# Post-norm transformer step with routed experts: norm, modulation, logits and choice of experts done token tile by token tile

## The reference

```python
xs = layer_norm(ALPHA * xs + g1 * y, ln1_g[l], ln1_b[l])
f = moe_ffn(xs * (1.0 + sc2) + sh2, w_router[l], b_router[l], w_expert_gu[l],
            w_expert_down[l], w_shared_gu[l], w_shared_down[l])
xs = layer_norm(ALPHA * xs + g2 * f, ln2_g[l], ln2_b[l])
```

```python
scores = jax.nn.sigmoid((x @ w_router).astype(jnp.float32))
sel = scores + b_router.astype(jnp.float32)
grp_score = lax.top_k(sel.reshape(t, N_GROUPS, N_EXPERTS // N_GROUPS), 2)[0].sum(-1)
_, gidx = lax.top_k(grp_score, TOPK_GROUPS)
gmask = jax.nn.one_hot(gidx, N_GROUPS, dtype=jnp.float32).sum(1) > 0
emask = jnp.repeat(gmask, N_EXPERTS // N_GROUPS, axis=1)
_, eidx = lax.top_k(jnp.where(emask, sel, NEG_INF), TOP_K)
```

## Time and profile before

| what | value |
|---|---|
| median of 3 runs | 2039.12 us (2036.37 to 2043.51) |
| the profiled execution | 2030.75 us, its span 2029.0 us |
| PE busy | 1544.4 us, 76% |
| DVE busy | 562.2 us, 28% |
| ACT busy | 317.1 us, 16% |
| POOL busy | 195.8 us, 10% |
| mean DMA rate | 284 GB/s |
| mean granted clock | 0.858 |

### The profile page before, as it was taken

One profiled execution on the slowest core, in us unless ns is written; L12 is line 12 of the kernel. 1 busy time (PEld: TensorE's weight loads), 2 busy tenths in 40 slices (PEclk: granted clock), 3 DMA queues, 4 the chain that ended last, 5 costly groups with the idle time before them and its releaser, 6 DMA issues. The chain is left out here.

```text
span 2029.0 us, 20342 instructions
## 1 busy us (share of the span) xinstructions
PE 1544.4 (76%) x7609; PEld 791.7 (39%) x7609; DVE 562.2 (28%) x1126; ACT 317.1 (16%) x620; POOL 195.8 (10%) x196
## 2 busy tenths in 40 slices
PE   3797888795976878877338979987958768788663
PEld 1685563542322323322116856645423323233221
DVE  0534435621110111101615253355201111111116
ACT  0322450110000000000012234411100000010000
POOL 0000000141010110110000000002401101111000
PEclk7898799697987988989768987996979888899887
DMA  7534418179999999996475344182799999999964
GB/s 291 189 108 165 170 22 322 69 252 424 411 408 417 408 403 390 401 424 239 186 278 160 125 148 163 42 325 77 283 423 405 416 406 397 415 398 397 403 243 173
DMA packets 114674, 576.90 MB, mean 284 GB/s; under 512 B 41644, under 2 KB 44220, under 8 KB 73480
## 3 DMA queue, kind: packets, MB, share of 16 engines
q1 hardware_dynamic: 93992, 534.35, 66.3%
q0 software_dynamic: 20512, 41.09, 5.4%
q10 hardware_dynamic: 64, 0.07, 0.0%
HBM read 565.09 MB, written 40.39 MB: 298 GB/s over the span
## 5 line engine op out<-in xcount | busy, mean ns | idle before, releaser
L993 PE MATMUL bank<-ring,arena_a 128*32 128x512 f32 (+2 forms) x2432 | 518.3, 691 | 218.0 <-DMA ring<-in_w_expert_gu 213.8
L993 PEld LDWEIGHTS bank<-ring,arena_a 128*32 128x32 f32 (+2 forms) x2432 | 175.4, 145 | 528.1 <-issue 527.1
L1017 PE MATMUL bank<-arena_b,arena_a 128*32 128x512 f32 (+2 forms) x800 | 207.4, 601 | 12.6 <-DMA arena_b<-in_w_expert_down 11.5
L1497 DVE SCALAR_TENSOR_TENSOR arena_a<-arena_a,slot_w,bank 128x256 f32<-128x256 f32 x64 | 30.8, 480 | 658.1 <-ACT arena_a L1737 631.8
L1737 ACT ACTIVATE arena_a<-bank 128x256 f32<-128x256 f32 x64 | 24.7, 385 | 915.5 <-PE bank L993 896.7
L1793 POOL DMA_INDIRECT scratch_y<-arena_a,slot_idx x64 | 63.6, 994 | 917.1 <-DVE arena_a L1514 915.9
L778 PE MATMUL bank<-win_hi,xmT_hi 128*128 128x512 f32 (+1 forms) x288 | 110.8, 385 | 26.0 <-DVE arena_a L1141 23.4
L1017 PE MATMUL bank<-arena_a 128*32 128x512 f32 (+2 forms) x416 | 116.0, 595 | 0.0
L1513 DVE COPY arena_a<-bank 128x512 f32<-128x512 f32 x64 | 44.3, 692 | 249.0 <-PE bank L1017 249.0
L779 PE MATMUL bank<-win_hi,xmT_lo 128*128 128x512 f32 (+1 forms) x288 | 111.2, 386 | 0.0
L780 PE MATMUL bank<-w_lo,xmT_hi 128*128 128x512 f32 (+1 forms) x288 | 110.7, 384 | 0.0
(11 more groups left out here) (266 smaller groups left out, 1667.2 us busy)
## 6 DMA issues: line engine op xcount, KB each, us to landing
ring<-in_w_expert_gu SPq DMA_DIRECT2D x128, 2048.0 KB
arena_b<-in_w_expert_down SPq DMA_DIRECT2D x88, 1024.0 KB, 22.3
ring<-in_w_mod SPq DMA_DIRECT2D x24, 2048.0 KB
arena_a<-in_w_expert_down SPq DMA_DIRECT2D x40, 1024.0 KB
ring<-in_w_in SPq DMA_DIRECT2D x10, 2048.0 KB
ring<-in_w_out SPq DMA_DIRECT2D x4, 2048.0 KB
ring<-scratch_y SPq DMA_DIRECT2D x4, 2048.0 KB, 10.8
ring<-scratch_y SPq DMA_DIRECT2D x8, 1024.0 KB, 17.1
```

Of the source, the lines that this page charges most:

```text
L993: ins = pe.matmul(psum[b % 2][r:r + w, :], xT[:, k, r:r + w], ring_view(gu_slot(n))[:, k, :], start=(k == 0), stop=(k == KD - 1))
L1017: ins = pe.matmul(psum[5 + f][r:r + w, :], hT[b % 2][:, k, r:r + w], down[n % ND][:, k, CH * f:CH * f + CH], start=(k == 0), stop=(k == 1))
```

## The change

The work is reordered by tiles; what is computed stays the same.

- `norm` takes a third argument, `follow`, and calls it for tile t right behind that tile's `scale_shift`. In the first norm this is the modulation, in the last norm the residual. Each waits for ScalarE's normalisation of its tile. ScalarE's `norm` is not changed.
- TensorE multiplies the logits of tiles 0 and 1 together into one bank, then turns tile 2 and multiplies its logits into another. ScalarE copies tiles 0 and 1, does their sigmoid, copies tile 2, does its sigmoid.
- `choose(t)` does the whole choice of one tile; every operation works on that tile alone. The mask's semaphore counts three, and TensorE waits for all three.

```diff
-                bank = begin(("logit",))
+                bank = begin(("logit", 0))
                 logits(bank, 0)
+                end(logits(bank, 1), ("logit", 0))
                 pe.wait_ge(xm_ready, TILES)
                 turn_x(1, 2, xm2)
-                logits(bank, 1)
-                end(logits(bank, 2), ("logit",))
-
-                pe.wait_ge(mask_ready, 1)
+                bank = begin(("logit", 1))
+                end(logits(bank, 2), ("logit", 1))
+
+                pe.wait_ge(mask_ready, TILES)
...
-                def norm(which, source):
+                def norm(which, source, follow):
 
                     for t in range(TILES):
                         statistics(t, source)
                         if t:
                             scale_shift(which, t - 1)
+                            follow(t - 1)
                     scale_shift(which, TILES - 1)
+                    follow(TILES - 1)
...
+                norm(0, from_psum, modulate_rows)
+
+                topv = top.rearrange("p (t g) e -> p t g e", t=TILES)
+
+                def choose(t):
+
+
+                    s8 = sel[:, t, 0:E].rearrange("p (g e) -> p g e", g=8)
+                    dve.wait_ge(score_ready, 1 if t < 2 else 2)
+                    link(dve.tensor_tensor(sel[:, t, 0:E], score[:, t], small[:, 0:E], ALU.add))
+                    for g in range(8):
+                        ins = dve.max(top[:, 8 * t + g, :], sel[:, t, 8 * g:8 * g + 8])
+                    link(ins)
+                    link(dve.tensor_tensor(grp[:, t, 0:8], topv[:, t, :, 0], topv[:, t, :, 1], ALU.add))
+                    link(dve.max(top8[:, t, :], grp[:, t, :]))
+                    link(dve.match_replace(grp2[:, t, :], top8[:, t, :], grp[:, t, :], MARK))
+                    link(dve.tensor_scalar(grp2[:, t, 0:8], grp2[:, t, 0:8], MARK, None, ALU.is_equal))
+                    link(dve.tensor_tensor(s8, s8, grp2[:, t, 0:8].unsqueeze(2).to_broadcast([P, 8, 8]), ALU.mult))
+                    link(dve.tensor_scalar(grp[:, t, 0:8], grp2[:, t, 0:8], -NEG, NEG, ALU.mult, ALU.add))
+                    link(dve.tensor_tensor(s8, s8, grp[:, t, 0:8].unsqueeze(2).to_broadcast([P, 8, 8]), ALU.add))
+                    link(dve.max(top8[:, t, :], sel[:, t, :]))
+                    link(dve.match_replace(sel2[:, t, :], top8[:, t, :], sel[:, t, :], MARK))
+                    dve.tensor_scalar(mask[:, t], sel2[:, t, 0:E], MARK, None, ALU.is_equal).then_inc(mask_ready, 1)
+                    dve.wait_ge(mask_ready, t + 1)
...
                 for t in range(TILES):
...
+                    choose(t)
...
-                norm(1, from_rows)
-                for t in range(TILES):
+                def residual_out(t):
+
                     dve.wait_ge(normal_ready, TILES + t + 1)
                     residual(t)
+
+                norm(1, from_rows, residual_out)
...
                 norm(0)
-                turned()
...
+                for t in range(TILES - 1):
+                    turned(t)
+                scored(0)
+                turned(TILES - 1)
+                scored(1)
```

More of the change, by code:

```diff
@@ L166, in psum_groups @@
     names += [("y", t, n) for t in range(TILES) for n in range(OUTC)]
-    names += [("xT", 1, t, g) for t in range(2) for g in range(2)] + [("logit",)]
-    names += [("xT", 1, 2, g) for g in range(2)]
+    names += [("xT", 1, t, g) for t in range(2) for g in range(2)] + [("logit", 0)]
+    names += [("xT", 1, 2, g) for g in range(2)] + [("logit", 1)]
     names += [("pos",), ("first",), ("rank",), ("where",)]
@@ L1339, in from_psum, with modulate_rows @@
                         dve.sem_inc(free[groups[("y", t, n)][0]], 1)
-                norm(0, from_psum)
-                for t in range(TILES):
+                def modulate_rows(t):
                     c_ = 0 if t == 0 else 1
@@ L1350, in _ @@
                 link(dve.memset(sel[:, :, E:E + 2], BIG))
                 link(dve.memset(grp[:, :, 8:12], BIG))
-                dve.wait_ge(score_ready, 1)
-                link(dve.tensor_tensor(sel[:, :, 0:E], score, small[:, 0:E].unsqueeze(1).to_broadcast([P, TILES, E]), ALU.add))
                 for t in range(TILES):
[L1355 to L1380, removed]
+                    choose(t)
                 link(dve.tensor_tensor(score, score, mask, ALU.mult))
@@ L1595, in _, with turned, scored @@
                 act.activation(lg, lg, ACT.Ln, bias=1.0).then_inc(softplus_ready, 1)
[L1597 to L1605, removed]
+                def turned(t):
+                    for g in range(2):
+                        name = ("xT", 1, t, g)
+                        bank = done(act, name)
+                        give(act.activation(xmT[:, 4 * g:4 * g + 4, P * t:P * t + P],
+                                            bank[:, :].rearrange("p (k t) -> p k t", k=4), ACT.Copy), name)
+                        act.wait_ge(free[groups[name][0]], groups[name][1] + 1)
+                        act.sem_inc(xmT_ready, 1)
+                def scored(g):
+                    at = slice(0, 2) if g == 0 else slice(2, 3)
+                    bank = done(act, ("logit", g))
+                    act.activation(score[:, at], bank[:, E * at.start:E * at.stop].rearrange("p (t e) -> p t e", e=E),
+                                   ACT.Sigmoid).then_inc(score_ready, 1)
+                    act.wait_ge(score_ready, g + 1)
+                    act.sem_inc(free[groups[("logit", g)][0]], 1)
                 def high_win(n, j):
```

## The result

The changed kernel took 2042.64 us (median of 20 runs, 2034.62 to 2049.09) against 2036.85 for the kernel before (median of 20, 2026.79 to 2043.51). The ratio is 1.0031, 95% interval [1.0017, 1.0046]: by it 6.3 us slower, between 3.5 and 9.4 (the two medians lie 5.8 apart). The forecast was +8.3 us (2047.4, range 2040.5 to 2051.5). The profiled execution took 2047.09 us with a span of 2045.0.

What follows compares the result with a forecast made beforehand. The bound was the chain of norm, modulation, logits and choice before the experts, and VectorE's last norm at each layer's end. Per layer 4.16 lost there and 0.0 before the experts, doubled, made +8.3 us: 2047.4, range 2040.5 to 2051.5.

Steps and rivals of the forecast that it cites:

- The tail: Last norm of each layer: three normalisations of 1.24 us no longer lie under other VectorE work; 4.16 us lost.
- The head: First norm to first use of the mask: later copies and smaller pieces pay back the overlap; nothing gained or lost.
- The clock: TensorE under the first logits: grant stays at 0.50 (1.2 GHz), so both tiles' logits take 7.04 us.
- Rival A: Clock up during both first logits, 2.0 us each: 3.0 gained before the mask, +2.3 in all, 2041.4; chance 0.15.
- The sum: Both layers' ends together: 2 x (4.16 + 0.0) = +8.3 us, giving 2047.4 from the median 2039.12.
- the chance of 0.62: Whole kernel slower by over 0.3% (6.1 us): 0.55 from the forecast itself plus 0.07 of B.
- B: Tile 2's copies wait behind ScalarE's first sigmoid, two more table loads, last scores decide: +12.5, 2051.6; chance 0.08.
- C: Last norm: moved work fills a wait because tile 2's rows come after 1000.7; +0.7, 2039.8; chance 0.05.
- D: Choice of experts: two thirds vanish, one piece behind tile 2's scores, 4.1 gained; +0.1, 2039.2; chance 0.04.

Runs made afterwards that it cites:

- tail-alone kernel: The kernel before with only the last norm changed, each residual right behind its tile's shift; 2048.28 us, ratio 1.0052.
- head-alone kernel: The changed kernel with the three residuals put back behind the whole last norm; 2035.57 us, ratio 0.9990.
- early version: The head-alone kernel with tiles 0 and 1 modulated before the third statistics and copied by ScalarE before tile 2's square root; 2018.64 us, ratio 0.9909.

## Why the prediction was right

**The tail** was the whole of the forecast: +4.16 us per layer predicted, 4.16 measured. The step that carried it, that tile 2's data lie ready and so the earlier residual fills no gap, held: TensorE had summed tile 2 at 1002.88 (997.46 + 5.42), VectorE came to it at 1008.95. The tail-alone kernel lost the time by itself (1.0052, where 1.0041 was expected), the head-alone kernel did not.

**The head** was put at nothing and gave 0.24 and 0.19 us. Its steps: the modulation of tile 2 ends 13.55 us behind the last bank, forecast 13.6; logits 7.06, forecast 7.04; one choice 3.37, forecast 3.36; the start of the first choice 19.20 behind the bank, forecast 19.56. The last makes the 0.3 us by which the head did better than its forecast: ScalarE finds all four turned banks ready and copies them in 2.72, some 0.71 apart and not 0.86, so the logits begin 0.34 us sooner than forecast. Nothing was gained because an earlier start of 2.92 us met 2.68 us for the smaller pieces, as the forecast has it.

**The clock** stood at the lower level, as taken from the earlier trace rows. Rival A's mechanism is real, though: with the clock held up the head gains 3.3 us (3.0 forecast). The changed kernel doesn't get there: TensorE stands idle for most of the time between the output projection and its logits, and the grant is 0.50 through the 7.06 us that they take. By the Trainium skill ("TensorE: Matmul & The Clock Gate", section "What's actually happening"), activity releases the throttle, and the logits should have gone over to the upper level on their way. This trace doesn't bear that out.

**The sum** was 8.3 us, the heads and tails of the traces say 7.9, the runs 6.3 with 3.5 to 9.4. The forecast of 2047.4 was 4.8 above the measured median; 2.3 of that is the base (2039.12 from three runs, 2036.85 from twenty). The time alone would not have told the forecast from rival A: its 2041.4 lies in the same range and nearer to 2042.64. What rules A out is the grant of 0.50 and the head of 29.34. And that the ratio lies above 1.003, the side with the chance of 0.62, is by a hair and owes something to luck; the interval reaches down to 1.0017.

What I had not reckoned with is that the head before is no constant. Where its clock rises late it is 2.9 us longer, and in the six layers seen with the new order and no transposes added the logits took 7.06 us each time. A late rise in the kernel before would move the comparison in the changed kernel's favour; by how much follows from how often it happens, which isn't settled. It can explain part of the step from 7.9 to 6.3, but the interval covers that step without it.

**Rivals B, C and D**: there was one sigmoid table load, under the logits (367.27), and none ahead of tile 2's copies (B); tile 2's rows came early (C); the choices didn't vanish (D). D's idea, one piece left behind the last scores, is what the early version does.

## What to carry to other kernels

Splitting a stage by tiles need not pay until every engine in the chain takes the tiles in the new order; look in the trace for ready data that lie waiting, here turned rows for 9 us, behind an engine's own older order. A dependent step moved right behind its producer on another engine exposes that engine's step each time (1.31 us here, 1.24 of it the normalisation), which pays only where the waiting engine was idle anyway. And small pieces have a price (here 10.14 us for three against 7.46 for one): the split gains only by what the first choice starts sooner beyond the 2.7 us that it costs. In the changed kernel that was 0.24 us; in the early order, where two of three choices lie ahead of the last scores, it was 3.9.

## What the runs showed of the hardware

- 32 products of 64 columns, each with its weight load, took 3.76 us at 2.4 GHz and 7.06 at 1.2 GHz. In all six layers of the changed order (changed kernel twice, head alone once) the grant was 0.50 from the first of them to the last. With transposes of the identity in the idle time ahead of them it was 1.00 from 350 to 368 us, with TensorE busy for 13.63 of these 18 us.
- In the kernel before, TensorE's last product of the output projection ended at 345.4 us and its next work began at 353.08. The grant was still 1.00 in the stretch to 350 and then fell (columns of the earlier trace rows):

```profile
349.00:350.00 1.00, 0.00 (x0) 0.00 (x0) 0.90 (x7) 0.59 (x2) 0.00 (x0) 1.00 0.87 360
350.00:351.00 1.00, 0.00 (x0) 0.00 (x0) 1.00 (x1) 1.00 (x2) 0.00 (x0) 0.56 1.02 360
```

- In the early version the logits begun 1.9 us behind the last bank, right after 1.91 us of turns, took 3.76 us.
- The rise comes at differing moments for the same program: in one execution one set of logits took 6.93 us in layer one and 4.04 in layer two.
- The stage with the experts differs by some us between executions of one kernel: 635.50 and 638.97 us from the mask to the last residual in layer two.
